# Delta stage on a later schedule, and sums of squares on four 64x64 tiles, in a fused two-layer decoder kernel

## What is computed

```python
# layer 0, 8 heads of 128, chunks of 64 tokens
q, k = l2_normalize(q), l2_normalize(k)            # sums of squares over a head's 128 channels
L = where(strict, (k*beta) @ k.T * decay, 0)       # per chunk
u, w = triangular_solve(eye + L, [v*beta, k*beta*exp(g)])
v_new = u - w @ state                              # chunk after chunk
o = q_dec @ state + a_qk @ v_new
state = state * g_last + k_dec.T @ v_new
o = rms_norm(o, norm_g) * silu(z)                  # sums of squares of o over 128 channels
# layer 1, 16 heads of 64
q, k = rms_norm(q, q_norm_g), rms_norm(k, k_norm_g)  # sums of squares over a head's 64 channels
probs = softmax(q @ k.T + c[t] - c[s], causal)
o = probs @ v * silu(z)
```

## Time and profile before

| | |
|---|---|
| median of three runs | 1855.02 us |
| the profiled execution | 1850.7 us, its span 1849.0 us |
| PE busy | 1736.6 us, 94% |
| DVE, ACT, POOL busy | 914.7, 754.0, 268.6 us |
| delta stage, heads in steady state | about 80.5 us an iteration |
| a step of three projection matmuls; with a block's products | 0.70 us; about 1.1 us |
| a step of the levels with its three projection matmuls | 1.78 us |
| attention stage, a pair in steady state | 55.35 us |

### The profile page before, as it was taken

One profiled execution on the slowest core, in us unless ns is written; L12 is line 12 of the kernel. 1 busy time (PEld: TensorE's weight loads), 2 busy tenths in 40 slices (PEclk: granted clock), 3 DMA queues, 4 the chain that ended last, 5 costly groups with the idle time before them and its releaser, 6 DMA issues. The chain is left out here.

```text
span 1849.0 us, 29061 instructions
## 1 busy us (share of the span) xinstructions
PE 1736.6 (94%) x11293; PEld 1315.6 (71%) x11293; DVE 914.7 (49%) x1736; ACT 754.0 (41%) x1232; POOL 268.6 (15%) x211
## 2 busy tenths in 40 slices
PE   7999999999999989879989999999999999899898
PEld 5777777777776777668877887666666666587687
DVE  3767575776757643754340210244444444565523
ACT  3436254453635462232231221455555555441411
POOL 2212122121212251210000000111111110012000
PEclk9999999999999989889989999999999999999899
DMA  5111110201101022122130110211111101041311
GB/s 129 46 47 42 29 36 24 47 14 46 46 24 35 24 93 91 35 86 80 41 113 4 46 47 20 46 41 44 37 37 43 34 28 44 1 171 35 114 43 49
DMA packets 113079, 92.86 MB, mean 50 GB/s; under 512 B 19696, under 2 KB 95664, under 8 KB 112944
## 3 DMA queue, kind: packets, MB, share of 16 engines
q1 hardware_dynamic: 112944, 91.02, 17.2%
HBM read 82.51 MB, written 8.49 MB: 49 GB/s over the span
## 5 line engine op out<-in xcount | busy, mean ns | idle before, releaser
L481 PE MATMUL gdn_unit<-part_hi,gdn_w_hi 128*128 128x512 f32 x512 | 233.9, 457 | 0.0
L483 PE MATMUL gdn_unit<-part_hi,gdn_w_lo 128*128 128x512 f32 x512 | 201.8, 394 | 0.0
L482 PE MATMUL gdn_unit<-part_lo,gdn_w_hi 128*128 128x512 f32 x512 | 201.0, 393 | 0.0
L2058 DVE CUSTOM_DVE_ANT_0 fa_probs<-fa_scores,fa_decay 128x896 f32<-128x896 f32 (+7 forms) x128 | 97.0, 758 | 122.4 <-PE fa_scores L1872 74.7
L872 DVE SCALAR_TENSOR_TENSOR x<-gdn_raw,gdn_taps,x 128x512 f32<-128x512 f32 x144 | 145.0, 1007 | 5.1
L446 POOL TENSOR_TENSOR gdn_w_lo<-ring,gdn_w_hi 128x1024 fp32r<-128x1024 f32 x31 | 78.0, 2516 | 308.7 <-ACT gdn_w_hi L673 308.2
L1824 PE MATMUL fa_unit<-part_hi,fa_w_hi 128*128 128x512 f32 x256 | 115.0, 449 | 4.9 <-ACT fa_qk L1971 3.4
L483 PEld LDWEIGHTS gdn_unit<-part_hi,gdn_w_lo 128*128 128x128 f32 x512 | 96.4, 188 | 21.5
L481 PEld LDWEIGHTS gdn_unit<-part_hi,gdn_w_hi 128*128 128x128 f32 x512 | 97.5, 190 | 16.7 <-issue 4.2
L2004 ACT ACTIVATE fa_probs_t<-fa_turned 128x512 f32<-128x512 f32 (+1 forms) x96 | 52.3, 545 | 139.1 <-PE fa_turned L1889 138.6
L1998 ACT ACTIVATE fa_probs<-fa_probs,fa_top 128x896 f32<-128x896 f32 (+7 forms) x128 | 99.4, 777 | 22.0 <-DVE fa_top L2058 18.1
(11 more groups left out here) (304 smaller groups left out, 3624.5 us busy)
## 6 DMA issues: line engine op xcount, KB each, us to landing
ring<-in_gdn_w_in_dram SPq DMA_DIRECT2D x32, 512.0 KB, 4.1
ring<-in_ple_w_gate_dram SPq DMA_DIRECT2D x32, 256.0 KB, 2.9
ring<-in_fox_w_in_dram SPq DMA_DIRECT2D x32, 256.0 KB, 2.9
ring<-in_fox_w_in_dram SPq DMA_DIRECT2D x16, 512.0 KB, 4.7
fa_decay<-c_rows_scratch SPq DMA_DIRECT2D x64, 128.0 KB, 3.0
in_x_tile<-in_x_dram SPq DMA_DIRECT2D x8, 512.0 KB, 6.4
gdn_g_bc<-g_rows_scratch SPq DMA_DIRECT2D x8, 512.0 KB, 8.7
x_scratch<-x SPq DMA_DIRECT2D x8, 512.0 KB, 2.9
```

Source lines behind the costliest of these rows:

```text
L481: pe.matmul(out, w_hi[:, j % 2, k, :], xh[:, k, ts], start=(k == 0), stop=False)
L482: pe.matmul(out, w_hi[:, j % 2, k, :], xl[:, k, ts], start=False, stop=False)
L483: mm = pe.matmul(out, w_lo[:, j % 2, k, :], xh[:, k, ts], start=False, stop=(k == KT - 1))
```

## The change

Two parts. In the delta stage the table moves `AT_FIRST`, `AT_VALUES` and `AT_LEVELS` (and so `AT_CHUNKS`, from 23 to 29), and the four positions of the output. In the attention stage the squares are laid out so that the two halves of the tokens of a head lie on different partitions: head 0's first half and head 1's second half stay where they were, ACT still squares these two (`quarter(n, n)`), and the other two quarters are squared by POOL (`cross`), which writes them to the other 64 partitions. PE's four matmuls then use the four 64x64 tiles of the array, one each, in place of two tiles twice, and wait for POOL's semaphore `crossed` as well.

```diff
 AT_KEYS = 3
-AT_FIRST = 8
-AT_VALUES = 9
-AT_LEVELS = 11
+AT_FIRST = 10
+AT_VALUES = 12
+AT_LEVELS = 17
 AT_CHUNKS = AT_LEVELS + 2 * LEVELS
-AT_O_TAKE = 35
+AT_O_TAKE = 41
...
-AT_O_SQUARES = 47
+AT_O_SQUARES = 53
-AT_O_SUMS = 53
+AT_O_SUMS = 59
-AT_O_NORM = 57
+AT_O_NORM = 62
...
+        def quarter(head, half):
+            at = half ^ head
+            return slice(half * DH, (half + 1) * DH), slice(at * HALF, (at + 1) * HALF)
+        def heads_half(p, kind, head, half):
+            return qk[head * DH:(head + 1) * DH, p % 2, kind, half * HALF:(half + 1) * HALF]
...
+            def cross(p, kind):
+                if p:
+                    pool.wait_ge(weighed, 4 * (p - 1) + 2 + kind)
+                pool.wait_ge(w_low, min(2 * p + 3, 2 * PAIRS))
+                for head in (1, 0):
+                    pool.wait_ge(unit_taken, 4 * p + 2 * kind + 2 - head)
+                    own = heads_half(p, kind, head, 1 - head)
+                    step(pool.tensor_tensor(squares[kind][quarter(head, 1 - head)], own, own, ALU.mult),
+                         None if head else crossed)
...
+                if it < PAIRS:
+                    cross(it, 0)
+                    cross(it, 1)
...
                 pe.wait_ge(squared, 2 * p + kind + 1)
-                for turn in range(2):
+                pe.wait_ge(crossed, 2 * p + kind + 1)
+                for half in range(2):
                     for head in range(2):
-                        rows, half = slice(head * DH, (head + 1) * DH), turn ^ head
-                        ts = slice(half * HALF, (half + 1) * HALF)
-                        mm = pe.matmul(scores[kind][rows, ts], c["ones"][rows, 0:DH], squares[kind][rows, ts],
-                                       start=True, stop=True)
+                        own, rows = quarter(head, half), slice(half * DH, (half + 1) * DH)
+                        mm = pe.matmul(scores[kind][head * DH:(head + 1) * DH, half * HALF:(half + 1) * HALF],
+                                       c["ones"][rows, 0:DH], squares[kind][own], start=True, stop=True)
...
-                step(act.activation(squares[kind], qk[:, p % 2, kind], ACT.Square), squared)
+                for n in range(2):
+                    step(act.activation(squares[kind][quarter(n, n)], heads_half(p, kind, n, n), ACT.Square),
+                         squared if n else None, ends=bool(n))
```

More of the change, by code:

```diff
@@ L1701, in fox_attention @@
         w_high, w_low, unit_made, unit_taken = sem("w_high"), sem("w_low"), sem("unit_made"), sem("unit_taken")
-        squared, summed, roots, normed = sem("squared"), sem("summed"), sem("roots"), sem("normed")
+        squared, crossed = sem("squared"), sem("crossed")
+        summed, roots, normed = sem("summed"), sem("roots"), sem("normed")
         masked, scored, topped, exped = sem("masked"), sem("scored"), sem("topped"), sem("exped")
```

## The result

The changed kernel takes **1821.1 us** (median of 4 executions, 1820.7 to 1822.8), the kernel before 1854.3 us (4 executions, 1852.7 to 1855.0). The ratio is 0.9824, with a 95% interval of 0.9807 to 0.9841: 33 us, 1.8% faster. The forecast was 1825 us with a range of 1816 to 1842, and a sum of -30.0 us. The profiled execution of after took 1821.1 us, with a span of 1819.4 us, 29.6 us less than before.

What follows compares the result with a forecast made beforehand. The prediction took PE's own queue to bound both stages, leaving only its idle time and its work to win. Delta stage -18.0 and attention -12.0 sum to -30.0 us: 1855.0 to 1825 us, range 1816 to 1842.

Steps and rivals of the forecast that it cites:

- The output's sums: Delta stage: PE's wait for POOL's addition falls from 2.30 to 0.26 us in six heads, -12.2 us.
- The clock: Delta stage: without the 2.3 us waits, PE's two 3.4 us stretches at the lower clock go, -3.0 us.
- The turns: Delta stage, AT_FIRST and AT_VALUES: waits for inv and att_t go except the last head's, -7.6 and -1.3 us.
- The cover: Delta stage, AT_FIRST: inv is 1.6 us early; where DVE loses more than that, the wait is back.
- What it adds: Delta stage, blocks 6 and 7: DVE's first tap meets POOL and delays rest, 0.6 us a head, +3.6 us.
- the old wait of 0.4 us stays: Delta stage, line 635 at step 36: the existing 0.4 us a head stays, as weights' steps keep their place against blocks.
- The tail: Delta stage, iteration 8 without projections: longer chain and filler waits, +2.5 us, between 0 and +5.
- the +1.0 for a longer low clock: Delta stage, iteration 8: the lower clock lasts longer in and behind the gaps, +1.0 us.
- Attention: Attention stage: sums of squares on four tiles -13.8 us, ACT's squares +1.8, together -12.0 us.
- The rival in which POOL takes 2.4 us, or four tiles don't overlap: Attention stage: POOL's squares take 2.4 us or four tiles don't run together at 512 columns, 1839 us; chance 0.10.

Runs made afterwards that it cites:

- `outputs_late`: The changed kernel with AT_FIRST, AT_VALUES, AT_LEVELS, AT_O_TAKE back at 8, 9, 11, 35; only the output's squares, sums and scaling stay late: 1853.0 us, ratio 0.9999.
- `blocks_13`: The changed kernel with the levels from step 13 instead of 17, AT_VALUES 11 and AT_O_TAKE 37: 1826.4 us, ratio 0.9860 to before.
- `squares_50`: `blocks_13` with AT_O_SQUARES at 50 in place of 53, so POOL adds before the low part: 1816.9 us, ratio 0.9803 to before.
- `squares_only`: The changed kernel with the old step numbers, so only the attention stage's squares and sums are changed: 1845.1 us, ratio 0.9958 to before.
- `turns_8`: The changed kernel with AT_FIRST back at 8 and AT_VALUES back at 9: 1835.6 us, ratio 0.9905 to before.
- `kind0_pool`: The changed kernel with all four 64x512 squares of q made by POOL, ACT making two of k alone: 1816.7 us, ratio 0.9800 to before.
- `same_bank`: The changed kernel with squares placed so that the two matmuls into one PSUM bank read different row tiles: 1821.5 us, ratio 0.9828 to before.

## Why the prediction came out right, point by point

- **The output's sums** (-12.2). The wait went to nothing, 0.0 in place of the 0.26 I had kept: 13.8 us for six heads. The cause was half told. I had written that the wait is made by ACT being busy with k when the output is ready; by `outputs_late` that order alone is worth nothing. What counts is the second half of the same step, the 7.7 us of blocks 6 and 7 between the sums of k and of the output. I had added them up as a check on ACT and not seen that they were the cover. `blocks_13` (12.9 us back) and `squares_50` (the same wait gone once the queue was 10.9 instead of 14.4 us) show it from both sides.
- **The clock** (-3.0). Right for the profiled execution, where two stretches in the heads are gone. By `squares_only` others have six. A stretch lengthens its head by less than the 1.7 us: the two heads of before that have one take 81.2 us instead of 80.5, since PE waits shorter for `inv` behind it. The term for `inv` was read from the same trace and has that in it already. This is a likely reason why the medians differ by 33.2 and the profiles by 29.6 us: the forecast's 4.3 us between profile and median of before were carried over to after, whose profile and median agree.
- **The turns** (-7.6 and -1.3). Both rows came out as written. The cover, reckoned as 1.6 us, measured 0.2 (`inv` at 561.73, PE at 561.93). From the end of the sums at 547.34 PE comes after 14.6 us, not 15.2, as the sums take 1.88 us and not 1.4. The root takes 4.0 us (3.8 assumed), and DVE from line 914 to `inv` 10.4 (9.8 assumed): line 907's first operation, beside POOL's line 466, takes 2.34 us in place of 1.64. Line 880's eight operations take 4.22 us beside POOL's addition, against 2.19 in `squares_50`, but cost nothing here, as DVE then still waits 1.14 us for the root. In `turns_8` the term is 7.1 us of `inv` and 1.3 of `att_t` against after, and its tail is longer too, which the sum did not have.
- **What it adds** (+3.6). The mechanism and the place were right: the tap takes 2.04 us, PE waits 1.0 us at line 635. The size was off. The new waits are 7.0 us in the place of 2.7, and 4.7 at line 629. That the total at line 635 came out at the forecast "about 7 us" is luck: the forecast was 0.4 old and 0.6 new a head, and it is 1.0 new and none old. The step that failed is "the old wait of 0.4 us stays, as the weights' steps keep their place against the blocks": they do in the program, but a low part starts when ACT has made the high part. Before, ACT's copy of the output at `AT_O_TAKE` (35) stood ahead of the high part of step 36 and held it until PE had made the output, and the tap had passed when POOL began. With `AT_O_TAKE` at 41 the high part (673) starts at 514.53, and the low part meets the tap one operation ahead of the state. Iteration 6 before, then after:

```profile
538.29 0.49 DVE L870 TENSOR_SCALAR x<-gdn_raw,gdn_taps 128x512 f32<-128x512 f32 x1
...
539.12 0.60 ACT L806 ACTIVATE o_t<-gdn_w 128x512 f32<-128x512 f32 x1 [3.14 <-PE gdn_w L640]
539.75 1.06 ACT L673 ACTIVATE gdn_w_hi<-ring 128x1024 fp32r<-128x1024 f32 x1
...
540.98 2.45 POOL L446 TENSOR_TENSOR gdn_w_lo<-ring,gdn_w_hi 128x1024 fp32r<-128x1024 f32 x1 [16.45 <-ACT gdn_w_hi L673]
```

```profile
515.76 2.39 POOL L446 TENSOR_TENSOR gdn_w_lo<-ring,gdn_w_hi 128x1024 fp32r<-128x1024 f32 x1 [16.85 <-ACT gdn_w_hi L673]
...
516.80 1.64 DVE L870 TENSOR_SCALAR x<-gdn_raw,gdn_taps 128x512 f32<-128x512 f32 x1
518.47 0.35 DVE L956 SCALAR_TENSOR_TENSOR gdn_state<-gdn_state,gates_last,gdn_w 128x128 f32<-128x128 f32 x1
...
518.88 0.49 PE L629 MATMUL gdn_w<-gdn_state,x 128*128 128x128 f32 x2 [0.65 <-DVE gdn_state L956]
```

`outputs_late`, with the blocks and `AT_O_TAKE` as before, has the 2.8 us at line 635 again; no run moves `AT_O_TAKE` alone. Net the new waits are +9.0 us, 5.4 more than the term.
- **What the sum lacked.** Each wait that goes also gives back what PE drains and fills around it. From the sums of k of iteration 1 to those of iteration 7 it took 484.5 us before and 463.5 now, 3.50 us a head. The waits account for 2.3 and the clock for 0.6; some 0.6 us a head remain, three waits that are no more. `turns_8` points the same way: with two waits more a head it is 1.64 us a head longer than after, of which its waits are 1.25. That it is the drain was only argued. It made up for the larger price: the delta stage gained 20.5 us where the sum had 18.0.
- **The tail** (+2.5). +4.1: 100.5 us from the sums of k of iteration 7 to the stage's end, now 104.6. The miss is in the first piece: from the projection behind the sums of k (633.1, and 608.57 now) to `AT_FIRST` 27.5 us became 29.6, where the forecast was 28.2. From there to the output's sums it is 59.9 and now 63.4 us, the +3.5 of the sum's terms (3.6 - 1.1 + 1.0), and from there to the end 1.5 us less (1.8 forecast). The wait ahead of the first filler, forecast at about 4, is 4.4. The +3.5 holds as a total only: the +1.0 for a longer low clock had the wrong sign (6.8 us of it behind the gaps, 10.2 before), and the levels start 11.2 us after `AT_FIRST`, where 9.0 was reckoned.
- **Attention** (-12.0). Four tiles do run together at 512 columns: the next group starts 0.85 us earlier, where I had put 0.86 and the other bound was 0. POOL's product of 64x512 takes 1.1 us (1.3 assumed), well hidden, and ACT's squares cost 0.16 us more a pair instead of 0.23. A middle pair has 1.53 us less (55.35 to 53.82), just the sum's 1.5. The first and the last gave 0.7 and 0.8 only: there PE has too little to do between the sums and the scores, and the roots and the scaling set the time (0.75 us for line 2124 at 1162.63). That is the 1.4 us between 12.0 and 10.6. The rival in which POOL takes 2.4 us, or four tiles don't overlap, is excluded, and `kind0_pool` shows that the remaining 0.31 us were ACT's.

The rule weighed against the trace, of the Trainium skill (TensorEngine Tiling (Array Packing), Restrictions and Gotchas, Gotcha 1), is not what decides here. `same_bank` has two different row tiles in each bank, and the trace shows the same 1.09 us and the same kernel time. It does so with different column tiles; two row tiles in the same column tile were not tried.

## What to carry to other kernels

When two reductions share one chain of engines, add up the whole queue from the first to the second and set it against the work that the waiting engine has in between; moving that work there can be worth more than any order of the queue, and shortening the queue does the same. A shift of steps moves every queue that it passes: look for which small transfer or copy stands behind a waiting instruction afterwards, as ACT's high parts did behind the turned values. And where a long operation of POOL can start beside a DVE operation on the critical path, expect that operation to end with POOL's, and look for it at every place where the two can meet.

## What the runs showed of the hardware

- A DVE operation of 0.49 us (`TENSOR_SCALAR`, 128x512 from SBUF to SBUF) that starts during an operation of POOL ends 0.28 to 0.29 us after POOL's end, whatever part of it is left: 2.04 us behind 536.61 (POOL until 538.37), 1.64 us behind 516.80 (POOL until 518.15). With POOL idle it takes 0.49. The Trainium skill (SBUF — State Buffer, SBUF: two separate sides) calls the port pair that the two engines share an exclusive lock and not a split of bandwidth; these rows agree in that the end follows POOL's, though the tap then needs only 0.28 us and not its own 0.49.
- POOL loses a little too: the same addition took 2.34 us before and 2.80 us in `outputs_late`, beside DVE's lines 872 and 880.
- Matmuls of 64x64 tiles with 512 columns in fp32 run four at a time: 1.09 us for eight, 1.93 us for two at a time, also when two row tiles write one bank, each in its own column tile (`same_bank`).
- After a wait of 2.3 us the granted clock of PE is at its lower level (1.2 GHz) for 3.4 us in some executions and not in others: six times in one, twice in another, behind the same waits.
